# Dense down products in seven parts, expert down weights in 16 KB runs, and four smaller rearrangements of a two-block transformer kernel

## The reference, cut to what matters

```python
# first block, layers 0 and 1 (D_FF = 2816): dense feed-forward, then a norm
gate, up = jnp.split(h @ ffn_w_gate_up[l], 2, axis=-1)
x = x + rms_norm((silu(gate) * up) @ ffn_w_down[l], post_ffn_norm[l])
# second block, layer 0 (D_FF = 2816): dense feed-forward
ff = (silu(h @ w_gate) * (h @ w_up)) @ w_down
h = layer_norm(ALPHA * h + ff, ln_g, ln_b)
# second block, layer 1: 8 experts of 3584 hidden units, the best 2 per token
top_val, top_idx = lax.top_k(h @ w_router, 2)
for e in range(8):
    y += weight[:, e:e+1] * ((silu(h @ w_gate[e]) * (h @ w_up[e])) @ w_down[e])
h = layer_norm(ALPHA * h + y, ln_g, ln_b)
```

## Time and profile before

| what | us |
|---|---|
| median of three timed executions | 2305.82 |
| lowest, highest | 2299.05, 2306.42 |
| the profiled execution, timed | 2305.74 |
| its span in the profile | 2304.0 |
| PE busy in the span | 2216.8 (96%) |
| VectorE, ScalarE, GpSimd busy | 692.4, 368.3, 107.8 |
| weights and other data read | 554.60 MB, 244 GB/s over the span |

### The profile page before, as it was taken

How to read it: one execution, slowest core, us unless ns; L and a number is a source line. 1 busy time by engine, 2 the same in 40 slices (tenths; PEclk the granted TensorE clock), 3 DMA queues, 4 the chain that set the end, 5 groups by cost and what they waited for, 6 DMA issues and landing times. The chain is left out here.

```text
span 2304.0 us, 35171 instructions
## 1 busy us (share of the span) xinstructions
PE 2216.8 (96%) x15127; PEld 1331.3 (58%) x15127; DVE 692.4 (30%) x1614; ACT 368.3 (16%) x947; POOL 107.8 (5%) x186
## 2 busy tenths in 40 slices
PE   8999999999999999999999999999899999989996
PEld 5878875779786666788757775333233233323322
DVE  3345543444443532345322624101110011101012
ACT  1520001241000141200011622100110011000000
POOL 3120000010000020100000200000000000000000
PEclk9999999999999899999999998999999999999998
DMA  9635433874535273353336245999999999999996
GB/s 313 221 91 174 147 126 132 175 226 147 183 110 165 82 249 130 102 183 137 125 110 221 69 155 188 368 368 405 409 404 409 405 408 405 409 401 409 402 409 230
DMA packets 196949, 564.52 MB, mean 245 GB/s; under 512 B 9832, under 2 KB 25384, under 8 KB 196792
## 3 DMA queue, kind: packets, MB, share of 16 engines
q1 hardware_dynamic: 187368, 536.95, 62.7%
q0 software_dynamic: 9424, 25.28, 3.8%
HBM read 554.60 MB, written 7.60 MB: 244 GB/s over the span
## 5 line engine op out<-in xcount | busy, mean ns | idle before, releaser
L2744 DVE TENSOR_TENSOR proj<-proj,ps_d 64x512 f32<-64x512 f32 (+2 forms) x32 | 22.0, 689 | 563.6 <-PE ps_d L1532 318.3
L1532 PE MATMUL ps_d<-slots,hT 128*32 128x512 f32 x1488 | 185.7, 600 | 5.9 <-DMA slots<-in_moe_w_gate 2.4
L1532 PE MATMUL ps_d<-slots,N 128*32 128x512 f32 x1344 | 167.8, 598 | 9.6 <-DMA slots<-in_moe_w_up 4.3
L1067 PE MATMUL ps_a<-hT,slots 128*128 128x256 f32 (+1 forms) x768 | 144.9, 350 | 1.8 <-ACT hT L1821 1.5
L1067 PEld LDWEIGHTS ps_a<-hT,slots 128*128 128x128 f32 x768 | 127.8, 194 | 19.6 <-issue 5.8
L1298 PE MATMUL ps_s<-slots,proj 128*128 128x512 f32 x264 | 121.6, 592 | 0.0
L1298 PE MATMUL ps_x<-slots,proj 128*128 128x512 f32 x264 | 121.6, 592 | 0.0
L1532 PEld LDWEIGHTS ps_d<-slots,hT 128*32 128x32 f32 x1488 | 52.2, 111 | 118.6 <-issue 114.4
L1532 PEld LDWEIGHTS ps_d<-slots,N 128*32 128x32 f32 x1344 | 47.4, 111 | 111.3 <-issue 106.2
L1042 PE MATMUL ps_a<-slots,hT 128*128 128x512 f32 (+5 forms) x320 | 107.2, 492 | 2.8 <-ACT hT L1821 2.8
L2037 ACT ACTIVATE PT<-ps_a 128x512 f32<-128x512 f32 x44 | 25.1, 596 | 422.7 <-PE ps_a L1624 422.6
(11 more groups left out here) (450 smaller groups left out, 3232.2 us busy)
## 6 DMA issues: line engine op xcount, KB each, us to landing
slots<-in_moe_w_gate SPq DMA_DIRECT2D x43, 2048.0 KB, 20.7
slots<-in_moe_w_up SPq DMA_DIRECT2D x42, 2048.0 KB, 22.9
slots<-in_moe_w_down SPq DMA_DIRECT2D x41, 2048.0 KB, 19.3
slots<-in_ffn_w_gate_up SPq DMA_DIRECT2D x20, 2048.0 KB, 9.3
late<-in_moe_w_up SPq DMA_DIRECT2D x14, 2048.0 KB, 20.9
late<-in_moe_w_down SPq DMA_DIRECT2D x14, 2048.0 KB, 19.8
late<-in_moe_w_gate SPq DMA_DIRECT2D x13, 2048.0 KB, 24.1
slots<-in_ffn_w_down SPq DMA_DIRECT2D x10, 2048.0 KB, 8.4
```

The source lines that it names most:

```text
L1067: last = pe.matmul(b[:, f * S + tokens.start:f * S + tokens.stop], v[:, k, part["c"] + P * f:part["c"] + P * f + P], lhs[:, k, tokens], st ...
L1532: last = pe.matmul(b[TILE * j:TILE * j + TILE, :], x[:, k, TILE * c:TILE * c + TILE], views[w][:, k % deep, 512 * h:512 * h + 512], start= ...
L2744: post(dve.tensor_tensor(hidden[low:high, half, :], gated[low:high, half, :], b[low:high, :], ALU.mult), *marks, *([("free", r, n)] if m = ...
```

## The change

**Dense feed-forward.** A new plan function `dense` lists all gate and up blocks first, then for each of the first four groups its down block and a block without a source ("sums", a slot that VectorE fills), then the down blocks of the last two groups. SyncE adds to the semaphore of such a slot when it is free and loads nothing. PE runs the gate and up of all eleven units, then for the first four groups the down product of 256 tokens, 512 hidden units and 1024 columns by seven products of 2x2 quarters (two matmuls of 128x512 each). Three products that go into a sum as they are add up in banks of rings "s" and "x"; four stand alone, in the four banks of rings "a" and "d". Then the plain downs of the last two groups run. VectorE forms the sums of weights and hidden units (`sum_down`); those of group 0 come after the hidden units of the last but one unit, ahead of the last unit's joins. ScalarE copies one of the alone banks, VectorE joins the four (`join_down`), and the norms add the joined parts.

**Router weights.** GpSimd loads them in its "pe" entry, into the buffer `small`; the router's linear product waits for that load, and there is no block for them.

**Late slots.** They take the fifth and sixth place of the cycle of eight, and their first loads wait for the odd layer's own attention in place of its cross attention, which writes one of its two buffers of probabilities into `proj` now.

**Down runs.** Partition p takes four rows in a row, 4p to 4p + 3 of a group's 512, one run of 16 KB (8 KB in the two half blocks at the end). The transposes of the hidden activations take every fourth column to match.

**Step order.** `early` is 2 in the last but one step as well.

```diff
+SEVENS = 4
+HOMES = (0, 1, 2, 3, None, None, 4, 5)
...
+    def dense(gate, up, down, width):
...
+        for c0 in range(0, width, 512):
+            w = min(512, width - c0)
+            groups.append({"gate": block(gv[:, :, c0:c0 + w], P, KD, w), "up": block(uv[:, :, c0:c0 + w], P, KD, w),
+                           "w": w})
+        for g, group in enumerate(groups):
+            c0, w = 512 * g, group["w"]
+            group["down"] = block(down[c0:c0 + w, :].rearrange("(k p) c -> p k c", p=P), P, w // P, D)
+            if g < SEVENS:
+                group["sums"] = block(None, P, 1, SLOT)
...
-        stage("ffn", groups=ffn(gu[:, 0:D_FF], gu[:, D_FF:2 * D_FF], a["ffn_w_down"][l], D_FF), loose=True,
+        stage("ffn", groups=dense(gu[:, 0:D_FF], gu[:, D_FF:2 * D_FF], a["ffn_w_down"][l], D_FF), loose=True,
...
-    stage("linear", lhs="hT", k=KD, blocks=columns(a["moe_w_router_2"][0], EXPERTS), dst="logits", loose=True,
+    stage("linear", lhs="hT", k=KD, blocks=[(None, 0, EXPERTS)], dst="logits", loose=True,
...
-                    src = w.rearrange("e (k p) c -> p (e k) c", p=P)[:, ks, cs]
+                    if name == "moe_w_down_2":
+                        g, k0 = divmod(ks.start, 4)
+                        src = w.rearrange("e (g p k) c -> p (e g) k c", p=P, k=4)[:, g, k0:k0 + ks.stop - ks.start, cs]
...
-                    sp.wait_ge(*lane.of(("turned", crossed, 1, 1)))
+                    sp.wait_ge(*lane.of(("turned", odd, len(stages[odd][1]["units"]) - 1, 1)))
+                    sp.wait_ge(*lane.of(("normed", odd, len(stages[odd][1]["sets"]) - 1)))
...
+                if src is None:
+                    sp.sem_inc(*lane.tick(slot_landed[slot_at(n)], ("weights", n), by=16))
+                    continue
...
+                                         (router, a["moe_w_router_2"][0].rearrange("(k p) e -> p k e", p=P)),
...
+            def down_sevens(group, g, pair, accs, alones):
...
+                (c11, c12), (c21, _) = accs
+                m1, m6, m5, m7 = alones
+                plain = [(c11, a12, b21), (m1, a11, b11)]
+                summed = [(c12, s4, b22), (c21, a22, t4), (m5, s1, t1), (m6, s2, t2), (m7, s3, t3)]
+                order = [plain[0], *summed[:2], plain[1], *summed[2:]] if g == 0 else [*plain, *summed]
...
+                    for k in range(2):
+                        last = pe.matmul(b[:, :], lhs[:, k, :], rhs[:, k, :], start=(g == 0 and k == 0),
+                                         stop=(alone_bank and g == SEVENS - 1 and k == 1))
...
+                pairs = [gate_up(group) if g else first_gate_up(group, s, stage_n) for g, group in enumerate(groups)]
...
+                for g in range(SEVENS):
+                    down_sevens(groups[g], g, pairs[g], accs, alones)
                 for t in range(T):
-                    down(*late[0], accs, False, False, [t], t == T - 1)
-                    down(*late[1], accs, False, True, [t], t == T - 1)
+                    for g in range(SEVENS, len(groups)):
+                        down(groups[g], g, pairs[g], accs, t)
...
-                        last = pe.transpose(b[:, f * P:(f + 1) * P], hidden[:, half, f * P:(f + 1) * P], ident[:, :])
+                        last = pe.transpose(b[:, f * P:(f + 1) * P],
+                                            hidden[:, half, :].rearrange("s (p f) -> s f p", f=4)[:, f, :], ident[:, :])
...
-                    early = 2 if many or len(late) < 2 else 1
+                    early = 2 if many or len(late) < 2 or q == len(steps) - 2 else 1
...
+                            if joint:
+                                part = parts_of[t][c]
+                                do(dve.tensor_tensor(part, part, b[:, :], ALU.add), ("free", r, n), sem=emptying[r])
...
+            def sum_down(group, g, p):
...
+                post(dve.tensor_tensor(t3, b22, b12, ALU.subtract), sem=down_summed)
+                do(dve.tensor_tensor(s1, a21, a22, ALU.add), sem=down_summed)
+                post(dve.tensor_tensor(b12, b12, b11, ALU.subtract), sem=down_summed)
+                do(dve.tensor_tensor(s2, s1, a11, ALU.subtract), sem=down_summed)
+                post(dve.tensor_tensor(t2, b22, b12, ALU.subtract), sem=down_summed)
+                post(dve.tensor_tensor(s3, a11, a21, ALU.subtract), sem=down_summed)
+                do(dve.tensor_tensor(s4, a12, s2, ALU.subtract), sem=down_summed)
+                do(dve.tensor_tensor(t4, b21, t2, ALU.subtract), ("down_summed", group["down"]), sem=down_summed)
...
+                        if i == len(units) - 2:
+                            sum_down(groups[0], 0, p0 + 1)
...
+                for g in range(1, SEVENS):
+                    sum_down(groups[g], g, p0 + 2 * g + 1)
+                join_down(stage_n)
```

More of the change, by code:

```diff
@@ L349, in cross @@
         groups = [dict(slots=2, dv=P, out=[(0, 2, "O", 256 * p)]) for p in range(2)]
[L350 removed]
+        stage("attend", preps=[], units=units, sets=groups, loose=True, **({"apart": True} if i else {}))
         attended = len(stages) - 1
@@ L504, in build @@
     past_slots = min([s["first"] for s in expert_stages], default=len(blocks))
-    crossed = max([s["attended"] for kind, s in stages if kind == "route"], default=None)
+    odd = max([n for n, (kind, s) in enumerate(stages) if kind == "attend" and "gated" in s["sets"][0]], default=None)
     memory_read = max([s["blocks"][0][0] for _, s in stages if s.get("lhs") == "memT"], default=None)
-    used_blocks = {b[0] for _, s in stages for b in s.get("blocks", [])}
+    used_blocks = {b[0] for _, s in stages for b in s.get("blocks", []) if b[0] is not None}
     for _, s in stages:
@@ L1286, in gate_up, with down @@
                 return state["pair"] - 1
-            def down(group, n_group, pair, accs, first, final, tiles=range(T), ends=True):
+            def down_sevens(group, g, pair, accs, alones):
+                slot(group["down"])
+                (b11, _, b21, b22), (a11, a12, _, a22), (t2, t3, t4), (s1, s2, s3, s4) = down_operands(group, g)
+                t1 = slot_view(group["down"])[:, 0:4:2, 512:1024]
+                (c11, c12), (c21, _) = accs
[3 more added lines that the diff above has]
+                order = [plain[0], *summed[:2], plain[1], *summed[2:]] if g == 0 else [*plain, *summed]
+                for i, ((r, b, n), lhs, rhs) in enumerate(order):
+                    alone_bank = (r, b, n) in alones
+                    if i == 0:
+                        pe.wait_ge(*lane.of(("hidden", pair)))
+                    if i == (1 if g == 0 else 2):
+                        pe.wait_ge(*lane.of(("down_summed", group["down"])))
+                    if g == 0:
+                        pe.wait_ge(*emptied(lane, r, n))
+                    for k in range(2):
+                        last = pe.matmul(b[:, :], lhs[:, k, :], rhs[:, k, :], start=(g == 0 and k == 0),
+                                         stop=(alone_bank and g == SEVENS - 1 and k == 1))
+                    done = [("used", group["down"]), ("used", group["sums"])] if i == len(order) - 1 else []
+                    if alone_bank and g == SEVENS - 1:
+                        last.then_inc(*lane.tick(filled[r], ("full", r, n), *done))
+                    elif done:
+                        last.then_inc(*lane.tick(down_done, *done))
+            def down(group, g, pair, accs, t):
                 v = slot(group["down"])
@@ L1293, in down @@
                         pe.wait_ge(*lane.of(("hidden", pair - (nf - 1) // 2 + f // 2)))
[L1294 to L1306, removed]
+                    for half in range(2):
+                        r, b, n = accs[t][half]
+                        fresh, stop = t == T - 1 and half and g == SEVENS and f == 0, g > SEVENS and f == nf - 1
+                        if fresh:
+                            pe.wait_ge(*emptied(lane, r, n))
+                        last = pe.matmul(b[:, :], hid[g][:, f, t * P:(t + 1) * P],
+                                         v[:, f, half * 512:(half + 1) * 512], start=bool(fresh), stop=stop)
+                        if stop:
+                            last.then_inc(*lane.tick(filled[r], ("full", r, n)))
@@ L1308, in ffn @@
+                if t == T - 1:
+                    if stop:
+                        lane.mark(("used", group["down"]))
+                    else:
+                        last.then_inc(*lane.tick(down_done, ("used", group["down"])))
             def ffn(s, stage_n):
                 groups = s["groups"]
[L1310 to L1320, removed]
-                        down(*late.pop(), accs, g == 1, False)
-                    late.append((group, n_group, pair))
```

110 lines of the change are left out of this document (81 added, 29 removed).

## The result

The changed kernel takes 2272.52 us (median of four runs, 2268.10 to 2273.84) against 2305.95 us for four runs of the kernel before: a ratio of 0.9865, 95% interval 0.9849 to 0.9881. The prediction was 2271 us, range 2262 to 2288, faster. Run again beside other kernels it took 2271.56 us (2268.49 to 2272.86), ratio 0.9878 (0.9861 to 0.9894). Its profiled execution has a span of 2270.0 us, 34.0 less than before.

A forecast was written before the change was run, and what follows sets the result against it. PE was taken to bound the kernel until 1515 us, DMA from then to 2275 us. Terms: 2305.74 - 20.6 (dense) - 12.0 (16 KB runs) - 1.9 (step order) = 2271.2 us; range 2262 to 2288.

The forecast's parts named there:

- rival D: Dense part: VectorE becomes the bound, one `sum_down` per feed-forward uncovered, 3 x 6.8 = 20.4 us, total 2292; chance 0.06.
- Tile 0's norm: First feed-forward: two more adds of 0.69 us fit a slack of 2.2 us; cost nothing, 1 us if it fails.
- 0.000625 us per run: Down loads: price per DMA run on top of 4.81 us per block; 128 runs make 4.89 us, 0.24 less.
- The line drawn through two points: Down loads: extrapolation from 2 KB runs (5.45 us per 2 MB) and 4 KB runs (5.13) to 16 KB, gaining 12.0 us.
- Rival B: Expert phase: 16 KB runs are not such for the engines, DMA stays at 406 GB/s, total 2283; chance 0.25.
- Rival C: Transposes of hidden activations: strided loads cost 1.26 us a turn, together 6.6 us, total 2278; chance 0.09.
- I take none, since PE keeps room: Strided transposes: no cost taken, as PE is idle 12.8 us in a pair of experts (219 us).
- 13.4 us per pair: Expert pairs: PE's room for longer transposes, 12.8 - 3.4 us of idle plus 4 us the clock could recover.
- E: Strided transposes: slower than before if a turn is over 2.1 us longer, loads six times as long; chance 0.03.
- After it the last step's up block sets the pace: Expert end: up block lands at 2266.0, its tiles began at 2267.95, so 1.9 us gained; bounds 6.9 gain, 2 loss.
- The 8.27 us before the late downs: Expert end: PE's wait for a down block, to be filled with 2 x 3.62 us of up tiles and gone.
- Nothing: Late slots: earlier loads gain nothing taken, as PE is at 98% from 1422 to 1515, at most 1.7 us there.

The follow-up runs named there:

- e6_sums_late: Changed kernel with VectorE's sums for the first seven-product group after the last unit's joins, not ahead of them: 2300.08 us, ratio 0.9986.
- e7_turns3: Changed kernel with each transpose of the hidden activations done three times in place of once, same result: 2283.54 us.

## Why the prediction was right, and where it was not

| term | forecast | measured |
|---|---|---|
| dense feed-forward | -20.6 | -20.6 |
| 16 KB runs, strided transposes with them | -12.0 | -9.2 |
| step order, late slots together | -1.9 | -0.4 |
| clock, not of the edit | 0 | -3.9 (-2.4 and -1.5) |
| sum | -34.5 | -34.1 |

**Dense.** Right to 0.1 us, and for the reason given: 24 matmuls fewer at 0.858 us while PE is the bound, with VectorE's 6.8 us where nothing else waits. e6_sums_late shows that the cover was real and what rival D would have been, only dearer: 28 us, not 20. Tile 0's norm, forecast to use 1.4 of 2.2 us of slack, left 0.85: ready at 368.33 + 1.29 = 369.62, taken at 370.47, answering to the earlier trace rows:

```profile
368.33 1.29 DVE L2347 SCALAR_TENSOR_TENSOR N<-X,stat,vec 128x1024 f32<-128x1024 f32 x1
```

```profile
370.47 1.04 PE L1073 MATMUL ps_s<-ident,N 128*128 128x128 f32 x8
```

**16 KB runs.** The mechanism was right and the size off. The mis-sized term is the price of a run, "0.000625 us per run": measured 0.00048 to 0.00056. The line drawn through two points from different stages had the right shape and a slope that was too steep, by 12 to 30% of the measured price. The windows rose to 412 GB/s as forecast; where only downs load, 429 were forecast, and the 5.7 us behind the last up block (2232.3 to 2238.0) show 424. Rival B (the runs are cut) is out: the changed kernel's packets and the step from 405 over 409 to 412 GB/s. The Trainium skill's preferred packet of 4096 bytes ("DMA: Bandwidth & Descriptors", section "SWDGE vs HWDGE vs iDMA") is no bound on the gain here; 8 and 16 KB both went faster. Nor are the 425 GB/s of its section "Bandwidth" contradicted: the stretch is a mixture in which only a third of the bytes changed.

**Strided transposes.** Rival C's mechanism exists, but a load takes one and a half times as long and not four times: 0.211 against 0.140 us. The step of the forecast held, "I take none, since PE keeps room". The room itself, put at 13.4 us per pair in rivals C and E, was too large: e7_turns3 makes it about 9 us, still far above the 11 x 0.09 = 1 us that the strides take of it. E needs loads six times as long and is out.

**Step order.** This step failed: "After it the last step's up block sets the pace [...] So 1.9 us". The block does set the pace: with the order alone in the kernel before, the tiles start as it lands, 1.4 us earlier. The step left out that the wait collected ahead of them ends with PE at 1.2 GHz, and that the last tiles pay for it, 1.7 us there: of the 2 us seen between the landing and the tiles, 1.4 could be had, and they went into that. In the changed kernel the tiles already start as the block lands without the order (0.94 us of waiting), so there is nothing to gain at their start, and the slow records remain, 1.4 us. The 8.27 us before the late downs are gone, as the forecast has it, but 6.36 us of waiting stand ahead of the last step's tiles instead.

**Late slots.** "Nothing", and it is nothing beside the new order. Whether the 1.9 us beside the old one are theirs, and through which slot's release they come, wasn't tried apart and stays open.

**Clock.** The forecast met 2272.5 partly by luck: terms too high by 4.3 us (2.8 + 1.5) were made good by 3.9 us of clock, which the kernel before shows in some executions too. It started from 2305.74 us, one of the slower executions of that kernel; what the edit itself is worth is nearer 30 us than the 34.5 of the sum. The timed runs scatter by more than that difference.

**One reading.** PE is not at eight or nine tenths in all 40 slices of the earlier trace rows: the last one, the end of the kernel, is at six. Nothing rests on it.

## What to carry to other kernels

Two edits of different regimes add up: count PE's instructions where PE is the bound, and the number of DMA runs where DMA is, with the price of a run taken from two lengths, of the same stage where there are such (from two stages it came out too high here). Before reordering work into a wait, ask which landing ends that wait, and what runs behind it at the lower clock: a loss ahead of another wait costs nothing, and one behind the last wait is paid. When an experiment comes out as expected, read the quantity that it varied as well. And lay two traces over each other at common marks; here the last stretch repeats to 0.4 us where the timed runs of the kernel before lie up to 8.6 us apart (2298.03 to 2306.65).

## What was not expected of the hardware

A weight load of 128 columns of float32 costs the same for a step of 8 bytes (0.209 us) as for one of 16 (0.211), against 0.140 for contiguous columns. The Trainium skill, "SBUF — State Buffer", section "Door 1: The DMA port swizzle", puts the full rate at two or more hits per line of 16 bytes; a step of 8 bytes has two, and here it isn't at the full rate, so for these loads the measurement differs from the rule.

A wait of PE of 6.4 to 6.6 us cost 1.4 and 1.7 us (end of the experts) and about 2.8 us (28.2 - 19.9 over three feed-forwards) beyond itself, with records of 1.07 us after it in place of 0.6; one of 3.86 us was followed by 1.7 us of the same loss.
